# Inputs turned by the host, first modulations in four groups, h and the first two weight blocks K-tile by K-tile

## The chip, the cores and the metric

The kernel runs on one core of a Trainium2 chip. The time is that of one execution on the device in microseconds (us). The five engines of the core run their own instruction lists and wait for one another by semaphores: TensorE (PE, with its weight loads shown as PEld), VectorE (DVE), ScalarE (ACT), GpSimd (POOL) and SyncE (SP). SP and POOL issue most of the DMAs.

## The reference

One inference step of a two-layer decoder trunk, for a prompt of 1024 tokens and 8 decoding samples with one token each (1032 tokens in all), in float32. Only its start matters here:

```python
c_gate_in = jax.nn.silu(c) @ mod_w[0] + mod_b[0]          # six modulations, each 1024 wide, per sequence
sh1, sc1, g1, sh2, sc2, g2 = ...
h = rmsnorm(x, norm_mix_pre[0]) * (1 + sc1) + sh1
b_gate, c_gate, v = split(h @ sc_w_in, 3)                 # 1024 -> 3 x 1024
y = causal_dwconv(c_gate * v, state, conv_w)
o = (b_gate * y) @ w_out
```

There are nine conditioning vectors c ("lanes"): one for the prompt, one for each sample. After this come the gated feed-forward layer, latent attention with a paged cache, and a second feed-forward layer.

## The kernel before

Activations lie turned: 128 partitions hold features, the free axis holds tokens, so x is `xT`, 8 K-tiles of 128 x 1032. Tokens are worked in three chunks of 344. Every matmul of weights is done in three passes of a split format (h_hi by w_hi, h_lo by w_hi, h_hi by w_lo), so each weight block of 128 outputs is first split by ACT (`w_hi`, a rounded copy) and DVE (`w_lo`, the rest), and so is h.

The start, in the order in which PE goes through it: x, c, the packed vectors and the states come as rows and are turned by PE, 128 x 128 at a time (the helper `trans`); ACT and DVE copy the turned tiles from PSUM to `xT`. ACT squares x, DVE adds the eight K-tiles per chunk, PE sums over the partitions (`token_sums`, L2671), DVE and ACT make 1 / root of it and PE spreads these over the partitions (`first_spread`). Between these stand eight products `mod_product(0..7)` (L2644): silu(c) by the first 2048 columns of the modulation weights, one K-tile of 128 x 2048 each, 1 MB. They give sh1 and sc1 together; then one row copy and one turn (`mod_turn(0)`). After that DVE makes `u = x * A * rs`, ACT makes `h_hi`, DVE makes `h_lo`, chunk by chunk, and inside a chunk K-tile by K-tile. PE follows with the first two weight blocks as a pair (`pair_tiles`, L2787 to L2789): per chunk and K-tile three matmuls for each of the two blocks, 144 in all. The two blocks give the c gate and v.

Then ACT copies the first result to `a_sb` (`conv_in`, L1436) and signals `a_e`; only then PE starts the third block (`up_part(b + 2, 0, ...)`, L2761 to L2763), since it writes the same PSUM banks. From there on the blocks of the stage follow, and after each block three of the 40 later products of modulations (`mods_after`), whose weights SP loads in four rotating buffers (`mod_late`).

`a_sb` lies on the memory of `xT`. So POOL first stores x to DRAM (`x_d`, three DMAs of 1.4 MB), and `a_sb` waits for these:

```python
pool.wait_ge(mod_mm, KD - 1)                  # POOL, ahead of the stores: seven of the first eight products done
...
if f == 0:
    act.wait_ge(x_saved, 16 * NU)             # ACT, ahead of conv_in of the first block
```

Behind the stores POOL issues eight small DMAs of the page table. DVE's `part` and SP's fifth weight block (n = 4) also wait for `x_saved`. The four first `mod_late` loads on SP wait for all eight products (`mod_mm` 8). All this order is written out by hand; no planner decides it.

Of the kernel before, what the change touches and what calls it, by code (L numbers as in the profile page):

```python
# [27 lines left out]
P = 128  # L28
# [139 lines left out]
def build(nc, ins, outs):  # L168
    (x_prompt, x_sample, cache_lat, cache_pe, page_table, mod_w, sc_w_in, sc_w_out, w_qa, w_qb, w_kva, w_kvb, w_o,
     ffn_w_in, ffn_w_out, w_kvbT, rope_tab, lanes, vectors, states) = ins  # L170
# [89 lines left out]
    def small(name, shape, dt=F32):  # L260
# [29 lines left out]
    x_in = at("x_in", [P, KT_TOK, D], A_H)  # L290
    mod_raw = [at(f"mod_raw{b}", [P, MH], o + i * MH * 4)
               for b, (o, i) in enumerate((o, i) for o in (A_W, A_H + KT_TOK * D * 4) for i in range(4))]
    mod_late = [at(f"mod_late{b}", [P, MH], A_A + 2 * KD * U4 + b * MH * 4) for b in range(4)]
    u8 = at("u8", [P, KD, UC], A_A)
    sqs = [at(f"sqs{i}", [P, UC], A_A + KD * U4 + i * U4) for i in range(2)]
    ss3 = [at(f"ss3_{i}", [P, UC], A_A + KD * U4 + (2 + i) * U4) for i in range(2)] + [ss_x]
    off = A_A + KD * U4 + 4 * U4
    mrow = [at("mrow0", [P, 2 * MG], off)]; off += 2 * MG * 4
    xs_in = at("xs_in", [NS, D], off); off += D * 4
    c_in = at("c_in", [MLANES, D], off); off += D * 4  # L300
    packs = at("packs", [P, 4, P], off); off += 4 * P * 4
    states_in = at("states_in", [2 * NS, D + 2 * F], off); off += (D + 2 * F) * 4
    mix_in, ffn_in = states_in[:, 0:D], states_in[:, D:D + 2 * F].rearrange("p (l d) -> p l d", l=2)
    csil = at("csil", [MLANES, D], off); off += D * 4
    ptmp = at("ptmp", [P, KF, NS], off); off += 1024
    assert off <= A_A + 2 * KF * U4
# [126 lines left out]
    with ExitStack() as ctx:  # L433
# [17 lines left out]
        vec_in, c_loaded, state_loaded = sem("vec_in"), sem("c_loaded"), sem("state_loaded")  # L451
        x_loaded, state_out = [sem("x_loaded0"), sem("x_loaded1")], sem("state_out")
        kq_h, kq_l = sem("kq_h"), sem("kq_l")
        csil_ready = sem("csil_ready")
        setup_t, setup_e = sem("setup_t"), sem("setup_e")
# [121 lines left out]
        def mod_tile(j):  # L577

            if j < KD:
                return mod_raw[j], j // 2, 32  # L580
            b = (j - KD) % 4
            return mod_late[b], b, 32 + 16 * ((j - KD) // 4 + 1)
# [30 lines left out]
        X_TURNS, X_HALVES = 2 * (KT_TOK + 1), KT_TOK + 1  # L613
        MOD_ROWS, MOD_PARTS, MOD_COLS = 6, 12, 16 * 12
# [131 lines left out]
        def _(sp):  # L746
# [6 lines left out]
            def load_mod(j):  # L753
                dst, b, _ = mod_tile(j)
                if KD <= j < KD + 4:
                    sp.wait_ge(setup_e, 3)
# [5 lines left out]
            sp.dma_start(c_in[:], lanes).then_inc(c_loaded, 16)  # L762
            for z in range(2):
                sp.dma_start(x_in[:, 4 * z:4 * z + 4, :], x_prompt[512 * z:512 * z + 512, :].rearrange("(t p) d -> p t d", p=P)
                             ).then_inc(x_loaded[z], 16)
            sp.dma_start(xs_in[:], x_sample).then_inc(x_loaded[1], 16)
            sp.dma_start(packs[:], vectors).then_inc(vec_in, 16)
            sp.dma_start(states_in[:], states).then_inc(state_loaded, 16)
            for j in range(KD):
                load_mod(j)  # L770
# [142 lines left out]
        def _(pool):  # L913
            pool.memset(ones[:], 1.0)
# [134 lines left out]
            pool.wait_ge(act_out, KT_TOK + 1)  # L1049
            pool.wait_ge(dve_out, KT_TOK + 1)  # L1050
# [101 lines left out]
        def _(act):  # L1152
# [13 lines left out]
            act.activation(csil[:], c_in[:], ACT.Silu).then_inc(csil_ready, 1)  # L1166

            for t in range(KT_TOK + 1):
                w = P if t < KT_TOK else NS
                act.wait_ge(pe_out, 2 * t + 1)  # L1170
                act.activation(xT[:, 0:4, t * P:t * P + w], bank(3 + 2 * t % 3).rearrange("p (k t) -> p k t", k=4)[:, :, 0:w],
                               ACT.Copy).then_inc(act_out, 1)

            def mod_evac(h):
                act.wait_ge(mod_mm, KD * (h + 1))
                act.activation(mrow[h > 0][:], bank(6 + h % 2), ACT.Copy).then_inc(act_psum, 1)
# [52 lines left out]
            act.wait_ge(act_out, KT_TOK + 1)  # L1229
            act.wait_ge(dve_out, KT_TOK + 1)  # L1230
            for c in range(NU):
                for m in range(KD):
                    square_x(c, m, xT[:, :, up_cols(c)], sqs)
            act.wait_ge(var_ready, NU)
            act.activation(t_root, t_var, ACT.Sqrt).then_inc(root_ready, NU)
            hi_to(1)
            mod_evac(0)
            for c in range(NU):
                for m in range(KD):
                    h_round(c, m, u8, mod(0, 0))  # L1240
# [489 lines left out]
        def _(dve):  # L1730
# [24 lines left out]
            dve.wait_ge(setup_t, 1)  # L1755
            dve.tensor_copy(csT[:], bank(1)[:, 0:KD * MLANES].rearrange("p (k c) -> p k c", k=KD)).then_inc(setup_e, 1)
            for t in range(KT_TOK + 1):
                w = P if t < KT_TOK else NS
                dve.wait_ge(pe_out, 2 * t + 2)
                dve.tensor_copy(xT[:, 4:8, t * P:t * P + w],  # L1760
                                bank(3 + (2 * t + 1) % 3).rearrange("p (k t) -> p k t", k=4)[:, :, 0:w]).then_inc(dve_out, 1)

            def taps(src, kt, w, dst):
                state = src.rearrange("p (m b k) -> p m b k", m=kt, b=NS)
# [7 lines left out]
            def vectors_in():  # L1772
                dve.wait_ge(setup_t, 2)
                for t, r in enumerate((125, 108, 66, 66)):
                    step(dve.tensor_copy(vec[:, t, 0:r], bank(0)[:, t * P:t * P + r]))
                settle()
                dve.wait_ge(setup_t, 5)
                taps(bank(2)[:, 0:2 * NS * KD], KD, v_scw, prev_mix[:])
                for l, src in enumerate((bank(2)[:, P:P + 2 * NS * KF], bank(1)[:, P:P + 2 * NS * KF])):
                    taps(src, KF, vec[:, 2 + l, :], prev_ffn[:, l])  # L1780
                dve.sem_inc(setup_e, 1)
# [7 lines left out]
            def mod_finish(h):  # L1789
                dve.wait_ge(mod_t, h + 1)  # L1790
# [3 lines left out]
                dve.wait_ge(dve_psum, 2 * (h + 1))  # L1794
# [139 lines left out]
            for c in range(NU):  # L1934
                for m in range(1, KD):
                    add_x(c, m, sqs, ss3[c])
# [5 lines left out]
            lo_to(1)  # L1942
            mod_finish(0)
            for c in range(NU):
                rs_in(c + 1)
                wait(dve, h_ready, c)
                A, B, x, rs_c, n = mod(0, 1), mod(0, 0), xT[:, :, up_cols(c)], bank((4, 5, 7)[c])[:, 0:UC], UC
                if c == NU - 1:
                    n = PL
                    modulate_s(c, x, u8, A, B, rs_c)  # L1950
                for m in range(KD + 1):
                    if m < KD:
                        dve.scalar_tensor_tensor(u8[:, m, 0:n], x[:, m, 0:n], A[:, m, 0:1], rs_c[:, 0:n], ALU.mult, ALU.mult
                                                 ).then_inc(u_ready, 1)
                    if m:
                        h_low(c, u8, B, [m - 1], hk_ready)
# [674 lines left out]
        def _(pe):  # L2631
# [4 lines left out]
            def mod_product(j):  # L2636
# [3 lines left out]
                if k == 0:  # L2640
                    wait(pe, dve_psum, 2 * (h - 1))
# [6 lines left out]
            def mod_turn(h):  # L2648
                pe.wait_ge(act_psum, h + 1)
                for i in range(4):  # L2650
                    ins = trans(bank(6 + h % 2)[:, i * P:(i + 1) * P], mrow[h > 0][:, i * P:(i + 1) * P])
                ins.then_inc(mod_t, 1)
# [7 lines left out]
            def first_stat(c):  # L2660
                pe.wait_ge(sx_added, 7 * (c + 1))
                token_sums(ps[0:RB, 3, UC + 4 * c:UC + 4 * c + 4], ss3[c]).then_inc(stat_ready, 1)

            def first_spread(c):
                pe.wait_ge(inv_ready, NU)
                spread(bank((4, 5, 7)[c])[:, 0:UC], 4 * c).then_inc(rs_ready, 1)
# [16 lines left out]
            for k in range(KD):  # L2683
                ins = trans(bank(1)[:, k * MLANES:(k + 1) * MLANES], csil[:, k * P:(k + 1) * P])
            ins.then_inc(setup_t, 1)
            for n in range(2 * (KT_TOK + 1)):
                t, half = n // 2, n % 2
                if n in (0, 8):
                    pe.wait_ge(x_loaded[n // 8], (16, 32)[n // 8])
                if n >= 3:  # L2690
# [712 lines left out]
```

## Time and profile before

| what | us |
|---|---|
| three runs | 2481.29, 2487.03, 2488.38; median 2487.03 |
| profiled execution, time | 2488.16 |
| profiled execution, span | 2486.4 |
| TensorE busy in the span | 2385.2 (96%) |
| mean granted TensorE clock | 0.986 of full |

The span runs from the first to the last instruction; all times below count from its start. The granted clock of TensorE has two levels, 1.0 (2.4 GHz) and 0.5 (1.2 GHz).

### The profile page before, as it was taken

The page shows a single profiled execution, that of the slowest core. Times are in us where ns is not written, and L with a number is a line of the kernel's source. Part 1 is how long each engine was busy: PE and PEld are TensorE (multiplying, and loading weights), DVE is VectorE, ACT ScalarE, POOL GpSimd, SP SyncE. Part 2 cuts the span into 40 slices and gives each one's busy share as a digit, 9 for nine tenths or more (in the row PEclk, how much of TensorE's full clock was granted, in tenths as well). Part 3 has the DMA queues.
Part 4 walks back from the last instruction along what each step waited for, and adds up shares of the span by engine and source line. Part 5 has one row for each costly group of instructions (what it writes and reads, how often), then busy time and mean ns, then how long its engine had stood idle before and what let it go on. Part 6 is the DMA issues. An engine that isn't in the chain of part 4 may idle for free. (4 is left out here: it accounts for less than half of the span.)

```text
span 2486.4 us, 44368 instructions
## 1 busy us (share of the span) xinstructions
PE 2385.2 (96%) x18745; PEld 2261.7 (91%) x18745; DVE 1670.7 (67%) x2594; ACT 947.8 (38%) x1654; POOL 204.3 (8%) x292
## 2 busy tenths in 40 slices
PE   7999999999999999999999999789989999999997
PEld 5888999989999999999985888559989999998997
DVE  5521326797777777687455666976797777777684
ACT  4211114543333335554343665024543333335442
POOL 1000000001111111000000000110001111111000
PEclk8999999999999999999999999899999999999998
DMA  9677323236766647666110032872237766647673
GB/s 347 223 269 262 110 98 118 97 123 175 193 170 170 159 153 264 201 218 210 51 39 17 22 149 81 345 278 101 101 123 176 193 168 172 159 155 255 203 236 125
DMA packets 111112, 416.92 MB, mean 168 GB/s; under 512 B 16249, under 2 KB 28809, under 8 KB 98338
## 3 DMA queue, kind: packets, MB, share of 16 engines
q0 software_dynamic: 38704, 211.83, 27.0%
q1 hardware_dynamic: 72210, 202.25, 24.3%
q8 instruction: 149, 2.44, 0.4%
q14 instruction: 49, 0.40, 0.0%
HBM read 359.61 MB, written 118.08 MB: 192 GB/s over the span
## 5 line engine op out<-in xcount | busy, mean ns | idle before, releaser
L2761 PE MATMUL ps<-h_hi,w_hi 128*128 128x344 f32 x816 | 263.8, 323 | 0.8 <-ACT a_sb L1436 0.8
L2763 PE MATMUL ps<-h_hi,w_lo 128*128 128x344 f32 x816 | 260.4, 319 | 0.0
L2762 PE MATMUL ps<-h_lo,w_hi 128*128 128x344 f32 x816 | 260.3, 319 | 0.0
L1747 DVE TENSOR_TENSOR d_lo<-d_raw,d_hi 128x768 fp32r<-128x768 f32 (+2 forms) x176 | 153.9, 887 | 76.4 <-ACT d_hi L1160 75.6
L1160 ACT ACTIVATE d_hi<-d_raw 128x768 fp32r<-128x768 f32 (+2 forms) x176 | 135.5, 787 | 133.9 <-DMA d_raw<-in_ffn_w_out 69.3
L1483 ACT ACTIVATE op_hi_Y<-op_raw_Y 128x512 fp32r<-128x512 f32 x80 | 50.5, 632 | 311.8 <-DVE op_raw_Y L2271 162.0
L2761 PEld LDWEIGHTS ps<-h_hi,w_hi 128*128 128x128 f32 x816 | 153.5, 188 | 5.4 <-issue 4.3
L2763 PEld LDWEIGHTS ps<-h_hi,w_lo 128*128 128x128 f32 x816 | 153.3, 188 | 0.0
L2762 PEld LDWEIGHTS ps<-h_lo,w_hi 128*128 128x128 f32 x816 | 153.2, 188 | 0.0
L2992 PE MATMUL ps<-s_hi_Y,op_hi_Y 128*128 128x258 f32 x640 | 129.8, 284 | 3.2 <-DVE v_sb L2277 1.9
L2992 PE MATMUL ps<-h_hi,op_hi_X 128*128 128x258 f32 x640 | 129.7, 284 | 2.4 <-DVE op_lo_X L2252 2.4
L2992 PE MATMUL ps<-s_lo_Y,op_hi_Y 128*128 128x258 f32 x640 | 129.8, 284 | 0.0
L2992 PE MATMUL ps<-h_hi,op_lo_X 128*128 128x258 f32 x640 | 129.6, 284 | 0.0
L2992 PE MATMUL ps<-h_lo,op_hi_X 128*128 128x258 f32 x640 | 129.6, 284 | 0.0
L2992 PE MATMUL ps<-s_hi_Y,op_lo_Y 128*128 128x258 f32 x640 | 128.6, 282 | 0.0
L983 POOL DMA_DIRECT2D act_d<-g_sb x52 | 41.4, 796 | 1043.6 <-DVE g_sb L2301 673.4
L1160 ACT ACTIVATE w_hi<-w_raw 128x1024 fp32r<-128x1024 f32 x54 | 56.5, 1057 | 146.5 <-DMA w_raw<-in_sc_w_in 131.7
L2217 DVE TENSOR_TENSOR a_sb<-a_sb,ps 128x1032 f32<-128x1032 f32 x8 | 9.8, 1230 | 140.8 <-PE ps L2763 140.8
L2992 PEld LDWEIGHTS ps<-s_hi_Y,op_hi_Y 128*128 128x128 f32 x640 | 98.9, 189 | 4.1 <-DVE v_sb L2277 2.4
L2992 PEld LDWEIGHTS ps<-h_hi,op_hi_X 128*128 128x128 f32 x640 | 99.4, 190 | 2.9 <-issue 2.9
L2992 PEld LDWEIGHTS ps<-h_hi,op_lo_X 128*128 128x128 f32 x640 | 100.0, 190 | 0.0
L2992 PEld LDWEIGHTS ps<-s_hi_Y,op_lo_Y 128*128 128x128 f32 x640 | 99.7, 190 | 0.0
(504 smaller groups left out, 7076.1 us busy)
## 6 DMA issues: line engine op xcount, KB each, us to landing
wsum_d<-in_ffn_w_out POOLq DMA_DIRECT2D x88, 704.0 KB, 10.5
mod_late<-in_mod_w SPq DMA_DIRECT2D x40, 1024.0 KB, 9.3
fr<-in_ffn_w_in SPq DMA_DIRECT2D x80, 512.0 KB, 4.4
d_raw<-in_ffn_w_out SPq DMA_DIRECT2D x72, 384.0 KB, 3.3
act_d<-g_sb POOLq DMA_DIRECT2D x52, 516.0 KB, 5.2
xc<-x_d POOLq DMA_DIRECT2D x10, 1376.0 KB, 8.2
w_raw<-in_sc_w_in SPq DMA_DIRECT2D x24, 512.0 KB, 3.7
d_raw<-wsum_d SPq DMA_DIRECT2D x32, 384.0 KB, 3.1
```

What stands on the lines that cost most here:

```text
L983: pool.dma_start(act_d[:, :, f, :].rearrange("c p t -> p c t"), g_sb[f % 2][:].rearrange("p (c t) -> p c t", c=NU)).then_inc(g_out[f % 2], 16)
L1160: act.activation(w_hi[k.slot][:, 0:k.kt, :], w_raw[k.slot][:, 0:k.kt, :], ACT.Copy).then_inc(hi_ready, 1)
L1483: act.activation(op_hi[op][:], fast_raw(op, i), ACT.Copy).then_inc(act_out, 1)
L1747: dve.tensor_tensor(w_lo[k.slot][:, 0:k.kt, :], w_raw[k.slot][:, 0:k.kt, :], w_hi[k.slot][:, 0:k.kt, :].bitcast(F32), ALU.subtract).then_i ...
L2217: dve.tensor_tensor(chunked(a_sb[:, 2:2 + T]), chunked(a_sb[:, 2:2 + T]), upset(1 - f % 2), ALU.mult).then_inc(mul_done, 1)
L2761: pe.matmul(o, w_hi[k.slot][:, t, :], h_hi[:, t, up_cols(c)], start=t == 0, stop=False)
L2762: pe.matmul(o, w_hi[k.slot][:, t, :], h_lo[:, t, up_cols(c)], start=False, stop=False)
L2763: ins = pe.matmul(o, w_lo[k.slot][:, t, :], h_hi[:, t, up_cols(c)], start=False, stop=t == KD - 1)
L2992: ins = pe.matmul(o[:, z, :], w[:, t, :], h[:, t, z * QT:(z + 1) * QT], start=op in ("X1", "Y6", "Z5") and t == 0 and n == 0, stop=t == KH ...
```

## The change

The host now gives x, the lanes, the vectors and the states already turned (`x_t`, `lanes_t`, `vectors_t`, `states_t`), so PE turns none of them. SP loads x by pairs of K-tiles; POOL loads the vectors and states at its start. The first 2048 columns of modulations are laid out by the host in four groups: group g has the shift and the scale for K-tiles 2g and 2g + 1, with all eight K-tiles of the product. Each group has its own product (32 matmuls of 128 columns), row copy, turn and finish on DVE. `mod_mm` is raised twice in a group, so it still reaches 8 at the end of the four. The statistics of x are made for all 1032 tokens at once, and the spread roots are copied to SBUF (`rs_sb`). DVE and ACT then make h for two K-tiles at a time and all tokens. PE goes through the pair of blocks in four parts of two K-tiles, 36 matmuls each, with the products of groups 2 and 3 between them. The first two weight blocks are loaded earlier (ahead of groups 1 to 3), the third and fourth behind group 2's product.

```diff
+            def load_group(g):
+                for i in range(2):
+                    sp.dma_start(mod_grp[g][:, 4 * i:4 * i + 4], mod_first[g, i]).then_inc(cols_in[g], 16)
+            sp.dma_start(c_raw[:], lanes_t).then_inc(c_loaded, 16)
+            for i in range(4):
+                sp.dma_start(xT[:, 2 * i:2 * i + 2, :], x_t[:, 2 * i:2 * i + 2, :]).then_inc(x_loaded[i], 16)
+            load_group(0)
+            for n in range(2):
+                load(n, sc_w_in[(D, 2 * D)[n] // P])
+            for g in range(1, 4):
+                load_group(g)
...
-                    if n == 0 or n == 2:
-                        sp.wait_ge(mod_mm, n + 2)
+                    if n < 2:
+                        continue
+                    if n == 2:
+                        sp.wait_ge(mod_mm, 6)
...
+            pool.dma_start(vec[:], vectors_t).then_inc(vec_in, 16)
+            pool.dma_start(st_in[:], states_t).then_inc(vec_in, 16)
...
-            pool.wait_ge(act_out, KT_TOK + 1)
-            pool.wait_ge(dve_out, KT_TOK + 1)
+            for i in range(4):
+                pool.wait_ge(x_loaded[i], 16)
             pool.wait_ge(mod_mm, KD - 1)
             for c in range(NU):
                 pool.dma_start(x_d[c], xT[:, :, up_cols(c)]).then_inc(x_saved, 16)
...
+            for k in range(KD):
+                if k % 2 == 0:
+                    act.wait_ge(x_loaded[k // 2], 16)
+                wait(act, sx_added, NU * (k - 2 if k > 2 else k - 1))
+                act.activation(sqs[k % 2][:], xT[:, k, :], ACT.Square).then_inc(sx_ready, NU)
...
+            act.activation(chunked(rs_sb[:]), upset(0), ACT.Copy).then_inc(rs_copied, 1)
             hi_to(1)
+            def group_out(g):
+                act.wait_ge(mod_mm, 2 * g + 2)
+                act.activation(grow[g % 2][:], bank(6 + g % 2)[:, 0:P], ACT.Copy).then_inc(grp_e, 1)
...
+            def group_h(g):
...
+                for i in range(2):
+                    dve.scalar_tensor_tensor(u[:, i, 0:TP], xT[:, k0 + i, 0:TP], A[:, k0 + i, 0:1], rs_sb[:, 0:TP], ALU.mult, ALU.mult
+                                             ).then_inc(u_ready, NU)
+                if g == 0:
+                    lo_to(1)
...
+            def group_product(g):
+                pe.wait_ge(cols_in[g], 32)
+                wait(pe, dve_psum, g - 1)
+                for k in range(KD):
+                    for a in range(4):
+                        ins = pe.matmul(bank(6 + g % 2)[32 * a:32 * a + MLANES, 0:P], csT[:, k, :], mod_grp[g][:, k, a, :],
+                                        start=k == 0, stop=k == KD - 1, skip_group_check=True)
+                    if k % 4 == 3:
+                        ins.then_inc(mod_mm, 1)
...
+            group_product(1)
+            group_turn(1)
             for n in (b, b + 1):
                 pe.wait_ge(w_ready, blocks[n].done)
-            for c in range(NU):
-                pair_tiles(b, b + 1, c, (KD - 1) * c, c)
+            for g in range(4):
+                group_pair(b, b + 1, g)
+                if g < 2:
+                    group_product(g + 2)
+                    group_turn(g + 2)
             pe.wait_ge(a_e, 1)
             up_part(b + 2, 0, range(NU))
```

Three places show how this moves instructions. The first is PE's list before, from the sixth product to the start of the pair; `ss_x` are the summed squares, `root_t` the roots, `mrow` the row copy of the modulations.

```order
L2644 MATMUL ps<-mod_raw_162,csT 9x256 [waits cols_in2]
L2644 MATMUL ps<-mod_raw_162,csT 9x256 x7
L2671 MATMUL ps<-ones,ss_x 86x1 [waits sx_added]
L2671 MATMUL ps<-ones,ss_x 86x1 x3
L2644 MATMUL ps<-mod_raw_163,csT 9x256 [waits cols_in3]
L2644 MATMUL ps<-mod_raw_163,csT 9x256 x7
L2634 MATMUL ps<-ident,root_t 128x86 [waits inv_ready]
...
L2634 MATMUL ps<-ident,mrow_174 128x128 [waits act_psum,setup_e]
L2634 MATMUL ps<-ident,mrow_174 128x128 x3
L2787 MATMUL ps<-h_hi,w_hi_71 128x344 [waits hk_ready,w_ready]
```

And PE's list now, from the first product to the product of group 3; `grow` is the row copy of a group, and the "..." stand for the other matmuls of the pair.

```order
L2690 MATMUL ps<-mod_grp_156,csT 9x128 [waits cols_in0]
...
L2690 MATMUL ps<-mod_grp_157,csT 9x128 [waits cols_in1]
...
L2709 MATMUL ps<-h_hi,w_hi_71 128x344 [waits hk_ready,w_ready]
...
L2690 MATMUL ps<-mod_grp_158,csT 9x128 [waits dve_psum,cols_in2]
L2690 MATMUL ps<-mod_grp_158,csT 9x128 x31
L2659 MATMUL ps<-ident,grow_167 128x128 [waits grp_e]
L2709 MATMUL ps<-h_hi,w_hi_71 128x344 [waits hk_ready]
...
L2690 MATMUL ps<-mod_grp_159,csT 9x128 [waits dve_psum,cols_in3]
L2690 MATMUL ps<-mod_grp_159,csT 9x128 x31
L2659 MATMUL ps<-ident,grow_168 128x128 [waits grp_e]
```

The products, all ahead of the pair before, now stand half ahead of it and half inside it. The seventh step of `mod_mm`, which was the product of `mod_raw_163` ahead of the pair, is the first half of the product of `mod_grp_159`, behind two of the four parts of the pair.

The second place is POOL's list from its start: before, nothing but constants stands ahead of the stores of x.

```order
L914 MEMSET ones 128x128
L915 MEMSET ident 128x128
L916 MEMSET mask_b 128x128
...
L1053 DMA x_d<-xT 1024x1x344 [waits dve_out,mod_mm,act_out,const_ready]
L1053 DMA x_d<-xT 1024x1x344 x2
L1055 DMA rows_153<-in_page_table 16x16x1 x8
```

Now:

```order
L917 DMA vec<-in_vectors_t 128x512
L918 DMA st_in<-in_states_t 128x832
L919 MEMSET ones 128x128
...
L1058 DMA x_d<-xT 1024x1x344 [waits x_loaded2,x_loaded3,x_loaded1,mod_mm,x_loaded0,const_ready]
L1058 DMA x_d<-xT 1024x1x344 x2
L1060 DMA rows_153<-in_page_table 16x16x1 x8
```

Two loads have come ahead, and the stores of x wait for the loads of x and, as before, for `mod_mm`.

The third place is ACT's list at the end of h, up to `a_sb`, before:

```order
L1176 ACTIVATE mrow_174<-ps 128x512 [waits mod_mm]
L1218 ACTIVATE h_hi<-u_169,modv 128x344 [waits u_ready] x16
L1211 ACTIVATE h_hi<-u_169 128x8x8 [waits u_ready]
L1218 ACTIVATE h_hi<-u_169,modv 128x336
L1218 ACTIVATE h_hi<-u_169,modv 128x336 [waits u_ready] x7
L1160 ACTIVATE w_hi_73<-w_raw_55 128x1024 [waits raw_ready2]
L1160 ACTIVATE w_hi_74<-w_raw_56 128x1024 [waits raw_ready3]
L1436 ACTIVATE a_sb<-ps 128x1032 [waits w_done,x_saved]
```

And now, from the row copy of the last group:

```order
L1241 ACTIVATE grow_168<-ps 128x128 [waits mod_mm]
L1249 ACTIVATE h_hi<-u_1_165 128x2x8 [waits u_ready]
L1250 ACTIVATE h_hi<-u_1_165,modv 128x1024
L1250 ACTIVATE h_hi<-u_1_165,modv 128x1024 [waits u_ready]
L1165 ACTIVATE w_hi_73<-w_raw_55 128x1024 [waits raw_ready2]
L1165 ACTIVATE w_hi_74<-w_raw_56 128x1024 [waits raw_ready3]
L1450 ACTIVATE a_sb<-ps 128x1032 [waits w_done,x_saved]
```

Row copies and rounds of h alternate now; `a_sb` keeps its place behind them and its two waits.

## Rows read from the trace of the kernel before

**Rows 1.** The page's first part: busy time, share of the span, instructions.

```profile
PE 2385.2 (96%) x18745; PEld 2261.7 (91%) x18745; DVE 1670.7 (67%) x2594; ACT 947.8 (38%) x1654; POOL 204.3 (8%) x292
```

**Rows 2.** By stretch: length, busy PE, PEld, DVE, ACT, POOL, clock, DMA share, GB/s.

```profile
9.00:13.20 4.20, 3.79 (x19) 3.79 (x20) 0.79 (x2) 1.19 (x2) 0.00 (x0) 1.00 1.03 415
...
37.10:47.30 10.20, 10.20 (x82) 5.83 (x80) 4.80 (x20) 2.92 (x4) 3.30 (x5) 0.51 0.80 318
47.40:50.70 3.30, 0.25 (x3) 0.01 (x1) 3.17 (x7) 0.51 (x2) 3.30 (x7) 0.96 1.01 329
50.80:57.50 6.70, 5.97 (x21) 6.00 (x22) 6.53 (x14) 3.96 (x7) 0.65 (x2) 0.52 1.01 355
57.60:77.00 19.40, 19.40 (x124) 19.04 (x122) 17.90 (x38) 11.01 (x19) 0.69 (x1) 1.00 0.60 224
78.00:200.00 122.00, 121.92 (x1015) 108.39 (x1016) 32.40 (x42) 17.84 (x21) 4.85 (x7) 1.00 0.72 264
```

**Rows 3.** Timeline of PE: start, us, line, form, count [idle before, releaser].

```profile
15.30 3.88 PE L2634 MATMUL ps<-ident,x_in 128*128 128x128 f32 x32 [0.36 <-DMA xs_in<-in_x_sample]
...
26.14 3.60 PE L2644 MATMUL ps<-mod_raw,csT 128*9 128x256 f32 x32 [2.25 <-DMA mod_raw<-in_mod_w]
...
32.87 0.77 PE L2671 MATMUL ps<-ones,ss 128*86 128x1 f32 x8
...
40.15 1.33 PE L2671 MATMUL ps<-ones,ss_x 128*86 128x1 f32 x8
...
45.83 1.38 PE L2634 MATMUL ps<-ident,root_t 86*128 86x86 f32 x8
...
51.53 0.63 PE L2787 MATMUL ps<-h_hi,w_hi 128*128 128x344 f32 x1 [3.88 <-DVE h_lo L1876]
...
78.08 0.42 PE L2761 MATMUL ps<-h_hi,w_hi 128*128 128x344 f32 x1 [0.79 <-ACT a_sb L1436]
```

**Rows 4.** Timeline of PE, the three later products behind the third block.

```profile
89.58 2.78 PE L2644 MATMUL ps<-mod_late,csT 128*9 128x256 f32 x48
```

**Rows 5.** PE's turns of x by form, 9 to 13 and 14 to 19.2 us.

```profile
L2634 PE MATMUL ps<-ident,x_in 128*128 128x128 f32 x17 | 3.8, 415 | 4.5 <-DMA x_in<-in_x_prompt 4.5
...
L2634 PE MATMUL ps<-ident,x_in 128*128 128x128 f32 x40 | 5.0, 279 | 0.4 <-DMA xs_in<-in_x_sample 0.4
```

**Rows 6.** Timeline of DVE.

```profile
33.55 3.62 DVE L1826 TENSOR_TENSOR ss_x<-ss_x,sqs 128x344 f32<-128x344 f32 x6 [0.56 <-ACT sqs L1189]
...
42.83 0.17 DVE L1811 SCALAR_TENSOR_TENSOR root_t<-root_t 86x12 f32<-86x12 f32 x1
...
46.64 2.36 DVE L1747 TENSOR_TENSOR w_lo<-w_raw,w_hi 128x1024 fp32r<-128x1024 f32 x2
...
84.94 1.28 DVE L2170 SCALAR_TENSOR_TENSOR y_sb<-a_sb,vec,y_sb 128x1024 f32<-128x1024 f32 x1
```

**Rows 7.** Timeline of ACT.

```profile
42.12 1.06 ACT L1160 ACTIVATE w_hi<-w_raw 128x1024 fp32r<-128x1024 f32 x1
...
45.97 0.60 ACT L1176 ACTIVATE mrow<-ps 128x512 f32<-128x512 f32 x1 [1.56 <-PE ps L2644]
...
77.02 1.01 ACT L1436 ACTIVATE a_sb<-ps 128x1032 f32<-128x1032 f32 x1
```

**Rows 8.** Timeline of POOL, the three stores of x.

```profile
44.00 2.81 POOL L1053 DMA_DIRECT2D x_d<-xT  x3 [41.97 <-PE ps L2644]
```

**Rows 9.** Waits of SP's queue: who for whom, total, times, longest.

```profile
SPq L837 <- DMA x_d<-xT: 17.2, 1, 17.2
```

**Rows 10.** The tile `x_d`, 0 to 120 us.

```profile
DMA to landing us min/median/max: 6.7/14.3/23.4
```

**Rows 11.** DMA queues, 46 to 52 and 54 to 66 us: packets, MB, share.

```profile
q0 software_dynamic: 477, 1.86, 100.8%
...
q1 hardware_dynamic: 450, 3.29, 65.3%
q0 software_dynamic: 451, 1.75, 35.7%
```

More of the change, by code:

```diff
@@ L760, in load_mod @@
                 sp.dma_start(dst[:], mod_src(j)).then_inc(cols_in[b], 16)
[L762 to L770, printed above, removed]
+            def load_group(g):
[9 more added lines that the diff above has]
+                load_group(g)
             def load_down(d, w):
@@ L1165, in _ @@
             act.wait_ge(c_loaded, 16)
[L1166 to L1172, printed above, removed]
+            act.activation(csT[:], c_raw[:], ACT.Silu).then_inc(csil_ready, 1)
             def mod_evac(h):
                 act.wait_ge(mod_mm, KD * (h + 1))
-                act.activation(mrow[h > 0][:], bank(6 + h % 2), ACT.Copy).then_inc(act_psum, 1)
+                act.activation(mrow[1][:], bank(6 + h % 2), ACT.Copy).then_inc(act_psum, 1)
             def root(q):
@@ L1754, in _ @@
             dve.sem_inc(setup_e, 1)
[L1755 to L1761, printed above, removed]
             def taps(src, kt, w, dst):
-                state = src.rearrange("p (m b k) -> p m b k", m=kt, b=NS)
+                state = src.rearrange("p m (b k) -> p m b k", b=NS)
                 for k, out in ((0, dst), (1, ptmp[:, 0:kt, :])):
@@ L1772, in vectors_in @@
             def vectors_in():
[L1773 to L1781, printed above, removed]
+                dve.wait_ge(vec_in, 32)
+                taps(st_in[:, 0:KD, :], KD, v_scw, prev_mix[:])
+                for l in range(2):
+                    taps(st_in[:, KD + l * KF:KD + (l + 1) * KF, :], KF, vec[:, 2 + l, :], prev_ffn[:, l])
             def mod(l, kind):
@@ L1932, in scale_tiles @@
                     dve.tensor_tensor(xc[:, m, 0:n], xc[:, m, 0:n], o_sb[:, m, 0:n], ALU.add).then_inc(x_new, 1)
-            for c in range(NU):
-                for m in range(1, KD):
-                    add_x(c, m, sqs, ss3[c])
+            for k in range(1, KD):
+                dve.wait_ge(sx_ready, NU * (k + 1))
+                wait(dve, sx_added, NU * (k - 1))
+                dve.tensor_tensor(ss_t[:], (sqs[0] if k == 1 else ss_t)[:], sqs[k % 2][:], ALU.add).then_inc(sx_added, NU)
             dve.wait_ge(stat_ready, NU)
@@ L1941, in _ @@
             vectors_in()
[L1942 to L1956, printed above, removed]
+            dve.wait_ge(rs_copied, 1)
@@ L1958, in act_lo_group @@
+            for g in range(4):
+                group_finish(g)
+                group_h(g)
             def act_lo_group(d, i):
@@ L2640, in mod_product @@
                 if k == 0:
-                    wait(pe, dve_psum, 2 * (h - 1))
+                    pe.wait_ge(dve_psum, max(4, 2 * h))
                 for g in range(8):
@@ L2658, in mods_after, with group_turn, group_pair @@
                     mod_turn(MOD_TURN[p])
-            def first_stat(c):
-                pe.wait_ge(sx_added, 7 * (c + 1))
-                token_sums(ps[0:RB, 3, UC + 4 * c:UC + 4 * c + 4], ss3[c]).then_inc(stat_ready, 1)
+            def group_product(g):
[7 more added lines that the diff above has]
+                        ins.then_inc(mod_mm, 1)
+            def group_turn(g):
+                pe.wait_ge(grp_e, g + 1)
+                trans(bank(6 + g % 2)[:, P:2 * P], grow[g % 2][:]).then_inc(grp_t, 1)
+            def group_pair(a, v, g):
+                for t in (2 * g, 2 * g + 1):
+                    if t < KD - 1:
+                        pe.wait_ge(hk_ready, NU * (t + 1))
+                    else:
+                        pe.wait_ge(h_ready, NU)
+                    for n, s in ((a, 0), (v, 1)):
+                        k = blocks[n]
+                        for c in range(NU):
+                            o = upset(s)[:, c, :]
+                            pe.matmul(o, w_hi[k.slot][:, t, :], h_hi[:, t, up_cols(c)], start=t == 0, stop=False)
+                            pe.matmul(o, w_hi[k.slot][:, t, :], h_lo[:, t, up_cols(c)], start=False, stop=False)
+                            ins = pe.matmul(o, w_lo[k.slot][:, t, :], h_hi[:, t, up_cols(c)], start=False, stop=t == KD - 1)
+                        if t == KD - 1:
+                            ins.then_inc(w_done, 1)
             def first_spread(c):
                 pe.wait_ge(inv_ready, NU)
-                spread(bank((4, 5, 7)[c])[:, 0:UC], 4 * c).then_inc(rs_ready, 1)
+                spread(upset(0)[:, c, :], 4 * c).then_inc(rs_ready, 1)
             def token_sums(out, src):
@@ L3372 @@
     arrays, ins, outs = {}, [], []
+    x = np.concatenate([inputs["x_prompt"][0], inputs["x_sample"][:, 0]])
+    lead = [("x_t", by_columns(x, KD))]
+    for name, a in lead:
+        arrays[f"in_{name}"] = a
+        ins.append(nc.dram_tensor(f"in_{name}", a.shape, F32, kind="ExternalInput").ap())
     for name in _INS:
```

167 lines of the change are left out of this document (81 added, 86 removed).

## The prediction

> **What bounds the kernel now.** I read the engine totals first: TensorE (PE) is busy 96% of the span, every other engine far less [rows 1]. The table by stretch then shows where the other 4% lie: from 78 us on PE is busy without a gap (121.92 of 122.00 us), while up to 57.5 us it idles or runs at a granted clock of 0.5 [rows 2]. So the change, which touches only the first 78 us, is worth what it does to one moment: the start of the third block of weights (`up_part(b + 2, ...)`), 78.08 us in the PE timeline [rows 3]. All behind it is the same work in the same order and shifts with it. The timeline shows that this block was released by ScalarE's (ACT) copy `a_sb`, which started at 77.02 and took 1.01 us [rows 7]. That copy waits for two things, the end of the pair of blocks (`w_done`) and the saved x (`x_saved`), because `a_sb` lies on the memory of `xT`. Before, the pair ended last: the three stores of x were issued from 44.00 [rows 8], the last landed 23.4 us after its own issue [rows 10], and SyncE (SP), which waits for the same semaphore, got it at the end of a 17.2 us wait [rows 9]. With the third issue near 45.7 (three issues in 2.81 us from 44.00) that is 69.1, eight microseconds ahead of the pair. The distance from the first issue to the last landing is 25.1 us.
>
> **The change, step by step** (times in the span; the sum is made against this execution).
>
> Loads. Before, 4.26 MB (c, x and the sample rows) had landed at 15.30, when PE began the last x tiles [rows 3]. Now 0.69 MB of tables (POOL's queue) come beside the same x: at the 415 GB/s of 9.0 to 13.2 us [rows 2] that is up to 1.7 us more, 16.9; none if they yield, 15.3. I take 16.9. The 72 transposes of x, the 4 of the tables and the 52 of the states go; they are off the new chain.
>
> Sum of squares. 8 squares of 1032 instead of 24 of 344; only the last pair of tiles is left when its data land: a square like an ACT copy of 1024, 1.06 us [rows 7], and two adds at 1.2 us (two w_lo subtractions of 1024 took 2.36 [rows 6]): 16.9 + 3.5 = 20.4. Before, the last add ended at 33.55 + 3.62 = 37.2 [rows 6].
>
> Token sums and roots. All twelve sums now stand in the chain: 1.33 us for four with PE at half clock [rows 3], some 3.8 us for twelve, to 24.2. From the end of the sums (40.15 + 1.33) to the last root instruction (42.83 + 0.17) went 1.5 us [rows 3, 6]: 25.7. Twelve spreads, eight being 1.38 [rows 3]: 2.1, to 27.8. Whether these run at half clock is open: PE does nothing ahead of them now. The clock column prints 1.00 for 9.0 to 13.2 [rows 2], yet the x transposes there took a mean of 415 ns against 279 ns for the same form later [rows 5], so the first matmuls did run slowly.
> The Trainium skill ("TensorE: Matmul & The Clock Gate", part 1) says that the throttled clock is the default and activity releases it; the durations agree with it and the column does not. By the column the sums would cost 3 x 0.77 = 2.3 us [rows 3] instead of 3.8, by the rule 3.8.
>
> First group. It multiplies as many columns as two of the old products, 3.60 us at half clock [rows 3]: 27.8 to 31.4; its weights landed long before (2.1 MB behind x). Meanwhile ACT copies the spread roots (1.0) and splits two weight blocks (2 x 1.06), to 30.9, so it is free. A copy of a quarter of the 0.60 us row [rows 7], the turn, and the handoffs: 0.8, to 32.2. On VectorE (DVE) five small steps (one of a few columns took 0.17 us [rows 6]) at 0.25 with their handoffs, 1.25; two `u` of 1024 columns at 1.2 (a like instruction took 1.28 [rows 6]); the two w_lo, 2.36, which stand ahead of the first h_lo; a small one and the first h_lo, 1.5: 39.8. The pair starts there, against 51.53 [rows 3]: 11.7 us earlier.
>
> Groups. PE idles ahead of it as it did before (47.4 to 50.7), so it starts at half clock again: 21 matmuls in 5.97 us, then 0.156 us each (124 in 19.40) [rows 2]. Group 0 has 36: 5.97 + 2.3 = 8.3, to 48.1. Product 2 at full clock: 48 matmul records took 2.78 [rows 4], a group's work is 32 of these, 1.8; copy and turn 0.8: 50.7. Group 1, 36 x 0.156 = 5.6: 56.3. Product 3: 1.8 to 58.1, turn 58.9, groups 2 and 3 11.2: 70.1. DVE and ACT need per group 1.25 + 2.4 for u and 2.7 for h_lo, about 6.5 us, under PE's 8.2, so they hide. The pair ends at 70.1 instead of 77.0: this is the 7 us that the reordering gives.
>
> The store of x. POOL still waits for `mod_mm` 7. That was the seventh of eight products, at 44.00 [rows 8]; now it is the first half of group 3's product, which stands in PE's order behind the matmuls of groups 0 and 1: 56.3 + 0.9 = 57.2. This is the step that decides: the pair got earlier by 7, the store later by 13. The 8 loads of late modulations are released 0.9 us behind it, as before 2.6 us behind it, four of 1 MB in flight at once. So I take the old duration whole, 25.1 us: x saved at 82.3. Bounds: alone the store moved 1.86 MB in 6 us [rows 11], so 4.23 MB are 13.6 us, and 17 with start and landing: 74. Beside the loads it moved 1.75 MB in 12 us [rows 11]; wholly so until 4.19 MB of loads are through (3.29 in the same 12 us, so 15.3), it would need about 27: 84. The nearest row is the old store with the same company.
>
> The new wait. ACT's `a_sb` waits until 82.3, ends at 83.3, and PE starts the third block there: 83.3 - 78.1 = +5.3 us. PE has then idled 13 us. After idling 3.3 us it had started at half clock and lost 5.97 - 21 x 0.156 = 2.7 us [rows 2]; I charge that again (before, the third block started at full clock): +8.0. Behind the wait on ACT stand the splits of later weights, on DVE `part` and the later w_lo, on SP the fifth weight block; none is needed before the third block has run for 11 us, where the old chain from `part` to y took 10 us, so they cost nothing. Removed instructions elsewhere save nothing on this path.
>
> Sum: 2488.16 + 8.0 = 2496.2 against this execution. It stands 1.1 us over the median of the runs shown (2487.03), so against that 2495.0. Under 0.3% (7.5 us) a measurement of this kernel can't tell from no change, and the forecast lies beside that line.
>
> **Rivals.**
> (a) The store isn't last: the pair's end decides, x is saved before 70.1, so the third block starts at 71.1: -7.0 us, 2480. It needs a store of 12.9 us; for it speaks that the loads beside it are issued later than it, against it the 25.1 us and even the 13.6 us of the undisturbed rate.
> The Trainium skill ("DMA: Bandwidth & Descriptors", on the anatomy of a GpSimd DMA) fits 2.0 us + bytes / 436 GB/s, which for the 4.23 MB is an estimate of 11.7 us and would bring exactly this; the trace has 310 GB/s alone and half of that in company, so it differs.
> (b) The store has less company (the loads queue behind it) and takes 18 to 20 us: saved at 76, third block at 77.3, and 2.7 for the clock: +1.9, 2489, not slower in any way that can be told. For it: before, no load moved a byte until POOL's issuing was over, as 46 to 52 us shows queue 0 alone [rows 11]. Against: the sharing followed all the same.
> (c) The gate opens later still: PE stays at half clock through groups 0 and 1, whose work comes in pieces with turns between. 51 more matmuls at 0.128 us extra are 6.5 us on the store: +14.5, 2501.5. For it: from 37.1 to 47.3 PE was busy all the time and the granted clock still 0.51; against: in the old pair the clock rose after 21 matmuls [rows 2].
>
> **How the numbers follow.** Forecast (the store ends between 79 and 85) 0.57, (a) 0.08, (b) 0.15, (c) 0.20. The forecast's own range is 2491 to 2499. Faster by over 0.3%: the lower half of (a) and a little for what I don't see, 0.07. Slower by over 0.3%: half of the forecast and all of (c), 0.49. Within 0.3%: the rest, 0.44. The range leaves out most of (a) and the upper part of (c): 2484 to 2503.
>
> **What would show it.** Right: ACT's `a_sb` waits for the DMA of `x_d`, not for PE; PE idles more than 10 us between the last matmul of the pair (near 70) and the third block (near 83), whose first 20 matmuls are at half clock; POOL's stores are issued near 57. Wrong: `a_sb` released by PE; stores issued before 50; or a store under 15 us. If the pair starts later than 42 the chain of squares, sums and roots was counted too short, and the whole moves with it, one for one.

## The result and the profile after

| kernel | median us | lowest to highest | runs |
|---|---|---|---|
| before | 2484.51 | 2478.02 to 2489.93 | 20 |
| after | 2491.70 | 2485.34 to 2497.15 | 20 |

The changed kernel is slower by the ratio 1.0031, 95% interval 1.0024 to 1.0039; the medians lie 7.2 us apart. The forecast was +8.0 us, which set against the 2484.5 of these runs would be 2492.5. The profiled execution of the changed kernel took 2494.17 us, its span 2492.3.

The first place to look is ScalarE's copy `a_sb`, which frees the PSUM banks for the third block, and what it waited for. These are three timelines of the kernel after: ACT, PE and POOL (start, us, line, form, count [idle before, releaser]).

```profile
81.44 1.03 ACT L1450 ACTIVATE a_sb<-ps 128x1032 f32<-128x1032 f32 x1 [16.58 <-DMA x_d<-xT]
```
```profile
82.52 0.66 PE L2777 MATMUL ps<-h_hi,w_hi 128*128 128x344 f32 x1 [13.13 <-ACT a_sb L1450]
...
96.74 2.78 PE L2669 MATMUL ps<-mod_late,csT 128*9 128x256 f32 x48
```
```profile
57.09 2.66 POOL L1058 DMA_DIRECT2D x_d<-xT  x3 [53.27 <-PE ps L2690]
```

Before, `a_sb` had no wait for a DMA and began at 77.02 [rows 7]; now ACT idled 16.6 us ahead of it until the store of x had ended, and PE idled 13.1 us. The third block begins at 82.52 against 78.08 [rows 3], +4.44 us. The 48 matmul records of the late products, which follow it in the same order in both kernels, begin at 96.74 against 89.58 [rows 4], +7.16: between the two, another 2.72 us went. The table by stretch of the kernel after shows on what (length, busy PE, PEld, DVE, ACT, POOL, clock, DMA share, GB/s):

```profile
71.60:82.50 10.90, 0.00 (x0) 0.00 (x0) 1.01 (x3) 1.03 (x1) 0.00 (x0) 0.50 0.86 311
82.50:88.50 6.00, 5.98 (x21) 5.98 (x22) 2.61 (x3) 2.76 (x3) 2.10 (x5) 0.50 0.83 298
88.60:200.00 111.40, 111.40 (x950) 97.86 (x949) 29.32 (x40) 13.39 (x16) 2.39 (x3) 1.00 0.68 251
```

PE was idle for over 10 us, the granted clock was at its lower level, and the third block's first 21 matmuls ran at that level for 6 us; before, the same block ran at 1.00 from its first matmul [rows 2]. From 88.6 on PE has no gap, so the 7.16 us stay.

The start itself became faster, as forecast. PE of the kernel after, from the token sums to the first matmul of the pair and the last group's product:

```profile
20.15 3.65 PE L2722 MATMUL ps<-ones,ss_t 128*86 128x1 f32 x24 [20.15 <-DVE ss_t L1938]
25.36 1.98 PE L2659 MATMUL ps<-ident,root_t 86*128 86x86 f32 x12 [1.57 <-DVE root_t L1812]
27.27 3.49 PE L2690 MATMUL ps<-mod_grp,csT 128*9 128x128 f32 x64
...
38.97 0.63 PE L2709 MATMUL ps<-h_hi,w_hi 128*128 128x344 f32 x1 [1.91 <-DVE h_lo L1975]
...
55.39 1.93 PE L2690 MATMUL ps<-mod_grp,csT 128*9 128x128 f32 x64
```

The pair starts at 38.97 instead of 51.53 [rows 3], 12.6 us earlier, and the timeline shows its last matmul beginning near 69.1. But POOL's store, 44.00 before [rows 8], is released by the first half of the product at 55.39 and is issued at 57.09.

What the store did then is read from the DMA queues of the kernel after, 56 to 62, 60 to 72 and 74 to 80 us (packets, MB, share of 16 engines; q0 carries the store, q1 the loads):

```profile
q1 hardware_dynamic: 121, 0.98, 57.8%
...
q0 software_dynamic: 1, 0.00, 0.2%
```
```profile
q1 hardware_dynamic: 474, 3.49, 70.9%
q0 software_dynamic: 384, 1.48, 29.9%
```
```profile
q0 software_dynamic: 574, 2.26, 103.2%
```

For the first 5 us behind its issue the store moved nothing; in the 12 us to 72 it got 1.48 MB beside 3.49 MB of loads, as in the old kernel (1.75 beside 3.29 [rows 11]); only when the loads were through did it run alone, 2.26 MB in 6 us. In company the two queues moved the same number of packets: 450 of the loads and 451 of the store from 54 to 66 us before [rows 11], 189 and 191 from 62 to 67 us after. A packet of the loads held 7.3 KB there before (3.29 MB by 450), one of the store 3.9 KB (1.75 MB by 451), so the loads got nearly twice the bytes. From the first issue to the start of `a_sb` it took 81.44 - 57.09 = 24.4 us, where I had 25.1.

### The profile page after: what moved, and what is told of

It is laid out like the page before. It is cut to its first block and busy times, and to the rows that moved or that the text cites. A ratio compares the mean times of both kernels' runs of the same rounds, so it can differ in the third digit from the quotient of the medians.

```text
span 2492.3 us, 44275 instructions
## 1 busy us (share of the span) xinstructions
PE 2366.4 (95%) x18737; PEld 2249.6 (90%) x18737; DVE 1660.5 (67%) x2551; ACT 935.5 (38%) x1620; POOL 203.2 (8%) x294
## 5 line engine op out<-in xcount | busy, mean ns | idle before, releaser
L2777 PE MATMUL ps<-h_hi,w_hi 128*128 128x344 f32 x816 | 265.0, 325 | 13.1 <-ACT a_sb L1450 13.1
```

The costliest lines, as they stand in the source:

```text
L2777: pe.matmul(o, w_hi[k.slot][:, t, :], h_hi[:, t, up_cols(c)], start=t == 0, stop=False)
```

## The experiments

My theory was: the loss is wholly the new wait for `x_saved`, made of a late issue of the store, its company on the DMA engines, and the lower clock that PE's idling brings. The rivals: the loss lies in the new layout itself (more work on VectorE or ScalarE, a pair that runs slower), or the store is slow whatever runs beside it. All five kernels start from the changed kernel. The first four ran on one chip beside 25 runs of the kernel before (median 2484.18), the fifth on another beside 11 (2483.89).

**The store earlier.** POOL waits for the fourth count of `mod_mm` and not the seventh, that is for the end of group 1's product and not for the first half of group 3's; nothing else moves.

```diff
-            pool.wait_ge(mod_mm, KD - 1)
+            pool.wait_ge(mod_mm, 4)
```

> The changed kernel with one edit: POOL's stores of x wait for the fourth instead of the seventh step of the products (end of group 1's product, near 33 us, instead of the middle of group 3's, 57 us). Theory (the store of x ends last and holds the third block): x is saved near 33 + 25 = 58, ahead of the end of the pair at 69.5; ACT's a_sb is released by PE, the third block starts near 70.6 at full clock, 7.5 us before the old kernel's 78.1, and the time is 0.3% under the old kernel (ratio 0.997), some 15 us under the changed one. Rival (the groups themselves cost the time, the store only happens to end there): third block near 82 as in the changed kernel, ratio 1.003. Second rival (the early store takes the loads of groups 2 and 3 with it): pair's products of groups 2 and 3 wait for DMA, pair ends later than 72.

Measured: 2476.89 us (2472.46 to 2479.15, 7 runs), ratio 0.9969, interval 0.9957 to 0.998. POOL, ACT and PE of this run, then two lines of its tile `x_d` (first and last issue; issue to landing):

```profile
33.31 2.66 POOL L1058 DMA_DIRECT2D x_d<-xT  x3 [29.47 <-PE ps L2690]
```
```profile
67.16 1.03 ACT L1450 ACTIVATE a_sb<-ps 128x1032 f32<-128x1032 f32 x1 [3.22 <-PE ps L2711]
```
```profile
38.27 0.63 PE L2709 MATMUL ps<-h_hi,w_hi 128*128 128x344 f32 x1 [1.83 <-DVE h_lo L1975]
...
68.31 0.36 PE L2777 MATMUL ps<-h_hi,w_hi 128*128 128x344 f32 x1
...
79.75 2.78 PE L2669 MATMUL ps<-mod_late,csT 128*9 128x256 f32 x48
```
```profile
L1058 POOL DMA_DIRECT2D x_d<-xT x3: 901/961/1069, 33.3 to 34.9; - x3
...
DMA to landing us min/median/max: 9.5/12.5/15.5
```

With the store issued at 33.31, `a_sb` is released by PE again, the third block follows the pair without an idle time, its first matmul takes 0.36 us and not 0.66, and the late products come at 79.75: 17.0 us earlier than in the kernel after and 9.83 earlier than before. One number changed, and the loss turned into a gain. So the layout costs nothing on this path, and the wait was the whole of the loss. The second rival, that the early store holds up the loads of groups 2 and 3, did not come either: the pair ends at 68.3, where it ended at 69.4 in the kernel after. The early store was also a shorter one than I expected: its last landing came 15.5 us behind an issue at 34.9, that is at 50.4, 17.1 us from the first issue and not 25, with the loads gone ahead of it once more (it moved nothing from 33 to 36 us) and the engines to itself from 40 to 46 us, 2.22 MB.

**The store without company.** The four `mod_late` loads that SP issues in front of its own wait for `x_saved` now go behind it.

```diff
                     if n == 4:
-                        for j in range(KD, KD + 4):
-                            load_mod(j)
                         sp.wait_ge(h_ready, NU)
...
                     load(n, sc_w_in[c // P + f])
+                    if n == 4:
+                        for j in range(KD, KD + 4):
+                            load_mod(j)
```

> The changed kernel with the four first late modulation loads (4 MB on SP) moved behind the wait for the saved x and behind the fifth weight block, so that the store of x has the DMA engines for itself. Theory (the store's 24 us are half company): with 310 to 375 GB/s as shown alone, 4.23 MB need 11 to 14 us and 3 for start and landing, x saved at 71 to 74, third block at 72 to 75.5, with or without the half clock at its start (+2.7): ratio to the old kernel 0.998 to 1.000. Rival (the store is slow by itself, its pieces being 1376 bytes): x saved near 80, ratio 1.002 or more. By the throughput of the queue in the changed kernel after the loads had ended (372 to 386 GB/s) I take 72.

Measured: 2482.5 us (2475.0 to 2488.16, 12 runs), ratio 0.999, interval 0.9979 to 1.0001. POOL, ACT and PE of this run:

```profile
56.02 2.66 POOL L1059 DMA_DIRECT2D x_d<-xT  x3 [52.19 <-PE ps L2691]
...
70.77 1.03 ACT L1451 ACTIVATE a_sb<-ps 128x1032 f32<-128x1032 f32 x1 [6.99 <-DMA x_d<-xT]
...
71.85 0.42 PE L2778 MATMUL ps<-h_hi,w_hi 128*128 128x344 f32 x1 [3.53 <-ACT a_sb L1451]
...
84.90 2.78 PE L2670 MATMUL ps<-mod_late,csT 128*9 128x256 f32 x48
```

Alone the store takes 70.77 - 56.02 = 14.75 us instead of 24.4: the company was some 9.6 us of it. The mechanism of rival (a), a short store, exists then, but even this store ends behind the pair: PE still idles 3.5 us. Nor is the store slow whatever runs beside it, as the rival had it: x is saved near 70.8, not near 80. The late products come 11.8 us earlier than in the kernel after: 9.6 by the shorter store, 1.07 by its earlier issue (56.02 against 57.09; group 0 of the pair took 7.12 us instead of 8.18, which this edit doesn't explain), and 1.17 because the third block lost less to the lower clock. By its interval this version can't be told from the kernel before. The Trainium skill ("DMA: Bandwidth & Descriptors", on the anatomy of a GpSimd DMA) fits 2.0 us + bytes / 436 GB/s for one DMA, which for the three as one is 11.7 us as an estimate; the run, with 14.75, shows it too short here even for a store without those loads.

**PE kept busy.** 74 matmuls whose result nothing reads fill PE's wait for `a_e`; the store and the order stay.

```diff
+            pe.wait_ge(dve_psum, 4)
+            pe.wait_ge(w_ready, blocks[b + 2].done)
+            for i in range(74):
+                pe.matmul(bank(6)[:, 0:UC], w_hi[blocks[b + 2].slot][:, i % KD, :], h_hi[:, i % KD, 0:UC], start=True, stop=True)
             pe.wait_ge(a_e, 1)
```

> The changed kernel with 74 matmuls of no use (third block's weights by h, into a PSUM bank that is free) between the pair and the wait for a_sb, so that PE works until near 81 us instead of idling 13 us. Theory (2.7 us of the loss are the half clock after the idle time): the third block starts at 82.5 as in the changed kernel but at full clock, and everything behind it is 2.7 us earlier; ratio to the old kernel 1.002 instead of 1.003. Rival (the slow start belongs to the wait, not to the clock): no change against the changed kernel, first matmuls of the third block at 0.29 us.

Measured: 2488.19 us (2485.18 to 2490.88, 11 runs), ratio 1.0015, interval 1.0006 to 1.0024. PE of this run, and its table by stretch from 82.6 to 86.3:

```profile
68.26 11.93 PE L2979 MATMUL ps<-h_hi,w_hi 128*128 128x344 f32 x74
82.64 0.47 PE L2777 MATMUL ps<-h_hi,w_hi 128*128 128x344 f32 x1 [2.45 <-ACT a_sb L1450]
...
95.69 2.78 PE L2669 MATMUL ps<-mod_late,csT 128*9 128x256 f32 x48
```
```profile
82.60:86.30 3.70, 3.66 (x13) 3.67 (x14) 0.39 (x1) 0.85 (x1) 2.10 (x5) 0.54 0.95 309
```

The dummies end at 80.2 and the third block still waits until 82.64, so the store's price is untouched, as the theory had it. The late products come 1.05 us earlier than in the kernel after, though, not 2.7: 2.45 us of idling were left, the granted clock stood at 1.00 through them and fell right behind, and 3.7 us of the third block ran at a mean of 0.54. Against the late products of before it is 82.64 - 78.08 = 4.56 for the start and 6.11 - 4.56 = 1.55 for the clock. The two ratios, 1.0031 and 1.0015, are too coarse to tell 1.05 from 2.7, and the 6.11 us of the trace, a ratio of 1.0025, lie just above this run's interval. Five executions taken together say more. From the first matmul of the third block to the late products is the same work in all of them:

| run | idle of PE ahead of the third block, us | to the late products, us |
|---|---|---|
| store earlier | 0 | 11.44 |
| before | 0.79 | 11.50 |
| PE kept busy | 2.45 | 13.05 |
| store alone | 3.53 | 13.05 |
| after | 13.13 | 14.22 |

So the extra time came in the three runs in which PE idled for 2.45 us or more, and it was shorter behind 2.45 and 3.53 us than behind 13.13. That all 2.7 us come back is shown only with the wait itself gone, in the first experiment; this run gave back 1.17 of them.

**Store and splits earlier.** To the first edit come three moves out of the chain to the pair: the first two weight blocks are loaded ahead of group 0, ACT splits both ahead of its wait for the roots, and DVE makes the `w_lo` of both ahead of the statistics and no longer between `u` and the first `h_lo`. So this run is set against the first experiment.

```diff
-            load_group(0)
             for n in range(2):
                 load(n, sc_w_in[(D, 2 * D)[n] // P])
-            for g in range(1, 4):
+            for g in range(4):
                 load_group(g)
...
+            hi_to(1)
             act.wait_ge(var_ready, NU)
...
+            lo_to(1)
             dve.wait_ge(stat_ready, NU)
...
-                if g == 0:
-                    lo_to(1)
```

> The early store of the first experiment, and the first two weight blocks loaded ahead of group 0 and split while ACT and DVE wait for the token sums, instead of between u and h_lo of group 0. Theory (the two w_lo subtractions, 2.36 us, stood in the chain to the pair): pair starts near 36.6 instead of 39.0, ends near 67.1, third block near 68.2; ratio to the old kernel 0.996. Rival (the chain is held elsewhere, by ACT's h_hi or the clock of PE): pair starts as before near 39 or PE's longer half clock eats it, ratio 0.997.

Measured: 2472.53 us (2467.88 to 2476.83, 5 runs), ratio 0.9947, interval 0.9932 to 0.9962. DVE of the first experiment, then DVE and PE of this run:

```profile
36.84 2.48 DVE L1975 SCALAR_TENSOR_TENSOR h_lo<-u,modv,h_hi 128x1024 fp32r<-128x1024 f32 x2
```
```profile
19.68 2.35 DVE L1760 TENSOR_TENSOR w_lo<-w_raw,w_hi 128x1024 fp32r<-128x1024 f32 x2
...
34.57 2.48 DVE L1973 SCALAR_TENSOR_TENSOR h_lo<-u,modv,h_hi 128x1024 fp32r<-128x1024 f32 x2
```
```profile
25.12 1.98 PE L2657 MATMUL ps<-ident,root_t 86*128 86x86 f32 x12 [1.57 <-DVE root_t L1811]
27.03 2.82 PE L2688 MATMUL ps<-mod_grp,csT 128*9 128x128 f32 x64
...
36.00 0.62 PE L2707 MATMUL ps<-h_hi,w_hi 128*128 128x344 f32 x1
...
65.34 0.36 PE L2775 MATMUL ps<-h_hi,w_hi 128*128 128x344 f32 x1
...
76.78 2.78 PE L2667 MATMUL ps<-mod_late,csT 128*9 128x256 f32 x48
```

In the kernel after and in the first experiment the two `w_lo` stood right ahead of `h_lo` (the DVE rows of the kernel after stand below). Now they run while PE makes the token sums. `h_lo` begins at 34.57 instead of 36.84 and the pair at 36.00 instead of 38.27, both 2.27 us earlier. So the term of 2.36 us for `w_lo` in the chain to the pair was rightly counted as being on the path. The late products come 2.97 us earlier (76.78 against 79.75): the other 0.7 us is group 0 of the pair, which took 7.26 us instead of 7.97, with fewer matmuls at the lower clock. This differs between executions without an edit to it (8.18 in the kernel after, 7.12 with the store alone).

**PE busy from the start.** To that, 60 matmuls whose result nothing reads go ahead of the token sums, so that PE has worked before its first needed instruction.

```diff
+            for i in range(60):
+                pe.matmul(bank(0)[:, 0:P], ident[:], ones[:], start=True, stop=True)
```

> The kernel of the run before it (the store of x issued after the fifth K tile of modulation group 0, the w loads and the splits of K tile 1 moved forward), and 60 matmuls of ones by the identity on TensorE into PSUM bank 0 ahead of the token sums, whose result nothing reads. What I hold: TensorE's first work in the kernel runs at the half pace only because nothing ran before it (24 sums in 3.65 us, 12 spreads in 1.98, product 0 in about 3.0), so with work before them the sums take about 1.9 us, the spreads about 1.0 and product 0 about 1.93; the first h_hi matmul of the pair comes 2 to 3.5 us earlier than in the run before it, the third block as much, and the ratio to the kernel before is 0.993 to 0.994. Rival 1: VectorE's and ScalarE's rounds on u, h_hi and h_lo and the landing of the weights bind the start of the pair, not TensorE: the sums get faster, the pair starts within 1 us of the run before it, ratio 0.9947. Rival 2: the added matmuls still run when the last sum of squares is ready at 20 us and delay the sums: ratio 0.995 to 0.996.

(The store's release is put wrongly there: it is the end of group 1's product, as in the first experiment.) Measured: 2469.94 us (2466.2 to 2474.49, 6 runs), ratio 0.9944, interval 0.9928 to 0.996. PE of this run, and its table by stretch:

```profile
20.00 1.93 PE L2720 MATMUL ps<-ones,ss_t 128*86 128x1 f32 x24
23.50 1.98 PE L2657 MATMUL ps<-ident,root_t 86*128 86x86 f32 x12 [1.57 <-DVE root_t L1811]
25.41 3.60 PE L2688 MATMUL ps<-mod_grp,csT 128*9 128x128 f32 x64
...
35.29 0.40 PE L2707 MATMUL ps<-h_hi,w_hi 128*128 128x344 f32 x1
...
64.73 0.36 PE L2777 MATMUL ps<-h_hi,w_hi 128*128 128x344 f32 x1
```
```profile
20.00:22.00 2.00, 1.93 (x26) 1.84 (x24) 2.00 (x2) 0.06 (x1) 0.00 (x0) 1.00 1.03 434
22.00:30.00 8.00, 6.11 (x85) 4.41 (x89) 3.27 (x15) 1.52 (x3) 0.00 (x0) 0.57 1.01 424
```

The sums took 1.93 us against 3.65, as I expected, and rival 2 did not come: they started at 20.00, against 19.91 without the added matmuls. The rest I had wrong: with the 1.57 us wait for the roots the granted clock was down again (0.57 as a mean from 22 to 30), the spreads took their 1.98 as before, product 0 took 3.60 against 2.82 in the run without the added matmuls, and the pair began only 0.7 us earlier. For the pair and the ratio the figures of rival 1 came out, but not its reason: what the sums saved came through to the spreads (23.50 against 25.12), and product 0 lost half of it again on PE. So PE's pace does bind the start, but the clock did not stay up. By the two ratios this version can't be told from the one before it; both beat the kernel before and the changed one.

## Why the prediction was right, step by step

The forecast's mechanism is what the profile after shows, and all three marks of it that I named are there: `a_sb` released by the DMA of `x_d`, PE idle for over 10 us, stores issued near 57. The sum compares like this:

| step | forecast | measured |
|---|---|---|
| token sums can start | 20.4 | 20.15 |
| twelve sums | 3.8 | 3.65 |
| twelve spreads | 2.1 | 1.98 |
| product 0 | 3.6 | 3.49 |
| pair starts | 39.8 | 38.97 |
| store issued | 57.2 | 57.09 |
| pair ends | 70.1 | 69.4 |
| store, issue to `a_sb` | 25.1 | 24.4 |
| third block starts, against before | +5.3 | +4.44 |
| lower clock behind it | 2.7 | 2.72 |
| whole | +8.0 | +7.16 at the late products, +7.2 between medians |

**Sum of squares: the right time by the wrong step.** I let the last two tiles wait for their data and then cost a square and two adds. The rows of the kernel after say otherwise (DVE, then ACT; the third DVE line is the `w_lo` of the splits):

```profile
8.57 1.23 DVE L1938 TENSOR_TENSOR ss_t<-sqs,sqs 128x1032 f32<-128x1032 f32 x1 [6.61 <-ACT sqs L1232]
11.93 8.07 DVE L1938 TENSOR_TENSOR ss_t<-ss_t,sqs 128x1032 f32<-128x1032 f32 x6 [2.13 <-ACT sqs L1232]
...
35.18 2.35 DVE L1761 TENSOR_TENSOR w_lo<-w_raw,w_hi 128x1024 fp32r<-128x1024 f32 x2
37.54 2.47 DVE L1975 SCALAR_TENSOR_TENSOR h_lo<-u,modv,h_hi 128x1024 fp32r<-128x1024 f32 x2
```
```profile
10.78 2.02 ACT L1232 ACTIVATE sqs<-xT 128x1032 f32<-128x1032 f32 x2 [2.32 <-DMA xT<-in_x_t]
...
17.36 1.06 ACT L1232 ACTIVATE sqs<-xT 128x1032 f32<-128x1032 f32 x1 [0.28 <-DVE ss_t L1938]
```

Six adds run back to back from 11.93 to 20.00, 1.35 us each, and the last squares on ACT wait for DVE to give a buffer back, not for x. So DVE's adds set the 20.0, counted from the second pair of x: ahead of the six, DVE idled 2.13 us for squares that had themselves waited 2.32 us for that pair. The last two pairs of x, which my sum waits for, set nothing; whether a faster second pair would move the 20.0, no run shows. That 20.4 came so near is luck.

**Pace of the first matmuls.** I took the lower pace for the sums (3.8 us) against the clock column. The column of the kernel after prints the full level there as well:

```profile
20.00:30.00 10.00, 8.29 (x88) 7.37 (x92) 3.26 (x14) 2.83 (x4) 0.00 (x0) 1.00 1.02 428
```

and the 24 records took 3.65 us. The fifth experiment settles it: the same 24 took 1.93 with work ahead of them. This is what the Trainium skill ("TensorE: Matmul & The Clock Gate", part 1) says, that the throttled clock is the default and activity releases it; the trace agrees by the durations.

**The issue of the store: two errors that cancel.** The product of group 3 began 0.9 us earlier than counted (55.39 against 56.3), but POOL's issue came 1.7 us behind its start and not 0.9: the sum has nothing for the way from the half product to POOL, some 0.7 us. Before, it was as long, from the end of the seventh product at 43.31 to 44.00.

**The store.** "I take the old duration whole" was right within 0.7 us, and for the reason given, the same company; the second experiment priced that company at some 9.6 us. My argument for rival (b), that the loads let the store go first, failed, since the order of the two queues was the reverse of before. The total hardly noticed; that it is the same bytes on the same engines, packet for packet while they share, fits this, but no run tried the other order alone. The upper bound of about 27 us doesn't follow from the figures beside it: 15.3 us with the loads, 6.5 for the remaining 2.0 MB at 310 GB/s and 3.4 for start and landing are 25.2.

**The rivals.** (a) needed a store done by the pair's end; even alone it was 3.5 us of PE's idling too late, and with the store moved earlier the third block starts at 68.31, where (a) said 71.1: the pair is through 1.8 us sooner than I counted, and `a_sb`, at 67.16, runs beside the pair's last matmuls and adds nothing behind them. (c), the lower clock through groups 0 and 1, did not come: in the kernel after, group 1 with the product behind it began at 49.57 and 55.39, 5.8 us apart where the full pace was counted as 5.6, and the product took 1.93 us, the full pace. That nothing queued behind the wait on ACT, DVE and SP would cost time held: PE has no gap from 88.6 to 200.

**What stays open.** The span of the one profiled execution grew by 5.9 us where the medians differ by 7.2. The traces show where it wanders: the same DMA issue of POOL (`act_d`) that stood at 369.70 us before stands at 376.86 after, 7.16 later, and up to 930 us its issues come 5.9 to 7.2 us later; behind that the distance runs between 6.0 and 12.5. The other runs wander there by several us too, so one execution's span is no check on the sum. What moves it was not followed. Nor was it found why the loads went ahead of the store in one kernel and behind it in the other.

## What to carry to other kernels

When a change lets a piece of work finish earlier, look at each semaphore that its steps raise for others: here a count that marked "nearly done" came to stand later in the new order, and a store that had been hidden by eight microseconds became the last thing to wait for; lowering that count from seven to four gave the gain. Price a transfer with the traffic that will run beside it, not by its rate alone, and charge the lower clock behind every wait that empties TensorE.

## What the runs showed of the hardware

- The store took 14.75 us alone and 24.4 beside the loads, with 1.48 of its MB moved in 12 us in company and 2.26 in 6 us once the loads were through.
- While a store and loads shared the DMA engines, both queues moved as many packets (450 and 451, 189 and 191), so the bytes went by the size of a packet. No run here changed that size.
- Of two queues issued within three microseconds of each other, the store's and the loads', one moved nothing for about 5 us: the loads before [rows 11], the store after.
- The clock fell with short pauses: 2.45 us of idling were followed by 3.7 us of the third block at a mean of 0.54, and 1.57 us, behind 24 sums of one column each, by spreads and a product at a mean of 0.57. In the first case it fell only behind the pause. Without a pause the third block ran at full pace from its first matmul (0.36 us).
- The granted clock as printed is not to be trusted for a kernel's first matmuls: 1.00 over 24 sums that took 3.65 us, and 1.00 over the same 24 in 1.93.
